# Output projection of a two-layer trunk: seven block products in place of eight, with weight sums made by accumulating transfers

## What is computed

```python
for l in range(DEPTH):                      # DEPTH = 2, S = 512 tokens, D = 1024
    h = rms_norm(x, norm_g[l])
    proj = jnp.einsum('bsd,de->bse', h, w_in[l])
    (a_u, a_v, a_z, b_q, b_k, b_v, b_z, i_q, i_k, i_w, g_a, g_b) = split_columns(proj)
    y_a = spatial_gating_branch(...)        # gated MLP over blocks of 128 positions
    y_b = sparse_attention_branch(...) * jax.nn.silu(b_z)
    o_a = jnp.einsum('bse,ed->bsd', y_a, w_oa[l])
    o_b = jnp.einsum('bse,ed->bsd', y_b, w_ob[l])
    merged = jax.nn.sigmoid(g_a + gate_b[l, 0]) * o_a + jax.nn.sigmoid(g_b + gate_b[l, 1]) * o_b
    x = x + jnp.einsum('bsd,de->bse', merged, w_out[l])     # the output projection: (512 x 1024) by (1024 x 1024)
```

## Time and profile before

| | |
|---|---|
| median of 3 runs | 811.78 us (810.96 to 811.89) |
| the profiled execution, its own time | 811.18 us |
| its span, first to last instruction | 809.4 us |
| TensorE busy | 791.1 us, 98% |
| VectorE busy | 552.2 us, 68% |
| ScalarE busy | 335.9 us, 42% |
| HBM traffic | 104 GB/s over the span |

### The profile page before, as it was taken

How to read it: one execution, slowest core, us unless ns; L and a number is a source line. 1 busy time by engine, 2 the same in 40 slices (tenths; PEclk the granted TensorE clock), 3 DMA queues, 4 the chain that set the end, 5 groups by cost and what they waited for, 6 DMA issues and landing times.

```text
span 809.4 us, 10691 instructions
## 1 busy us (share of the span) xinstructions
PE 791.1 (98%) x3868; PEld 665.5 (82%) x3868; DVE 552.2 (68%) x987; ACT 335.9 (42%) x642; POOL 91.3 (11%) x85
## 2 busy tenths in 40 slices
PE   3999999999999999999999999999999999999998
PEld 2988888888888888888889888888888888888886
DVE  2878999978766753466268799999786567434821
ACT  3656645341444323432254675433324342434400
POOL 1137520000000000000011764000000000000000
PEclk9999999999999999999999999999999999999999
DMA  8535232323233122254062522323322223125211
GB/s 303 183 110 174 82 92 67 103 79 104 78 105 101 47 86 80 95 192 139 32 199 89 183 79 79 104 80 104 102 81 78 82 75 104 53 79 202 84 53 53
DMA packets 38309, 85.26 MB, mean 105 GB/s; under 512 B 2672, under 2 KB 2864, under 8 KB 38256
## 3 DMA queue, kind: packets, MB, share of 16 engines
q1 hardware_dynamic: 34496, 71.31, 27.9%
q0 software_dynamic: 3472, 12.67, 5.0%
q10 hardware_dynamic: 288, 0.59, 0.2%
...
HBM read 78.27 MB, written 6.29 MB: 104 GB/s over the span
## 4 chain that ended last, share of the span: by engine, by line
PE 91%; DVE 6%; DMA 1%; ACT 1%; issue 1%; ACTq 0%; DVEq 0%
PE bank L563 25%; PE bank L561 25%; PE bank L562 25%; PE bank L613 4%; PE bank L535 2%; PE bank L553 2%; PE bank L491 1%; DMA eye<-in_ident 1%; PE bank L544 1%; PE bank L506 1%; PE bank L505 1%; DVE w_lo L920 1%; PE bank L476 1%; DVE index_lo L920 1%; PE bank L647 0%
## 5 line engine op out<-in xcount | busy, mean ns | idle before, releaser
L561 PE MATMUL bank<-h_lo,w_hi 128*128 128x512 f32 x448 | 180.6, 403 | 0.0
L563 PE MATMUL bank<-h_hi,w_hi 128*128 128x512 f32 x448 | 174.7, 390 | 0.0
L562 PE MATMUL bank<-h_hi,w_lo 128*128 128x512 f32 x448 | 174.4, 389 | 0.0
L920 DVE TENSOR_TENSOR w_lo<-w_raw,w_hi 128x1024 fp32r<-128x1024 f32 x120 | 155.4, 1313 | 13.0 <-ACT w_hi L689 8.5
L561 PE MATMUL bank<-w_lo,h_hi 128*128 128x512 f32 x384 | 150.4, 392 | 0.0
L563 PE MATMUL bank<-w_hi,h_hi 128*128 128x512 f32 x384 | 149.8, 390 | 0.0
L562 PE MATMUL bank<-w_hi,h_lo 128*128 128x512 f32 x384 | 149.7, 390 | 0.0
L689 ACT ACTIVATE w_hi<-w_raw 128x1024 fp32r<-128x1024 f32 x120 | 123.2, 1055 | 8.4 <-ACT probs L830 3.7
L562 PEld LDWEIGHTS bank<-h_hi,w_lo 128*128 128x128 f32 x448 | 84.2, 188 | 18.6 <-issue 1.4
L561 PEld LDWEIGHTS bank<-h_lo,w_hi 128*128 128x128 f32 x448 | 84.2, 188 | 18.3 <-issue 1.4
L563 PEld LDWEIGHTS bank<-h_hi,w_hi 128*128 128x128 f32 x448 | 84.1, 188 | 17.9
...
...
## 6 DMA issues: line engine op xcount, KB each, us to landing
w_raw<-in_w_in SPq DMA_DIRECT2D x96, 512.0 KB, 3.7
w_raw<-in_w_out SPq DMA_DIRECT2D x16, 512.0 KB, 3.3
out<-x_sb POOLq DMA_DIRECT2D x4, 1024.0 KB, 5.3
w_raw<-in_w_oa SPq DMA_DIRECT2D x8, 512.0 KB, 3.3
w_raw<-in_w_ob SPq DMA_DIRECT2D x8, 512.0 KB, 3.4
x_sb<-out POOLq DMA_DIRECT2D x2, 2048.0 KB, 8.2
x_sb<-in_x SPq DMA_DIRECT2D x4, 512.0 KB, 9.7
...
```

The source lines that it names most:

```text
L561: nc.tensor.matmul(dst, s_h, m_l, start=(n == 0), stop=False)
L562: nc.tensor.matmul(dst, s_l, m_h, start=False, stop=False)
L563: last = nc.tensor.matmul(dst, s_h, m_h, start=False, stop=(n == len(pairs) - 1))
L920: nc.vector.tensor_tensor(lo, w_raw[:, n % RAW], hi.bitcast(F32), ALU.subtract) \
```

## The change

With the merged matrix A in four blocks (tokens 0 to 255 and 256 to 511, by inner rows 0 to 511 and 512 to 1023) and the weights B in four blocks of 512 x 512, the output is made from seven block products instead of eight, in Winograd's form of Strassen's scheme. In the names of the program: a11 and a12 take blocks of A as they are, s5, s6, s3 and s4 take sums and differences of blocks of A, and a22 again a block. In the order a11, a12, s5, s6, s3, s4, a22 each product is two jobs of 12 matmuls (one for each tile of its 256 tokens), so out has 14 jobs, which I number 0 to 13. Some are added into a bank that an earlier product left there, and so wait until VectorE has read it: s6 on s5, s3 on a11, s4 on s3, a22 on s4.

The sums of weights are made in `w_raw`. A product has two units of 512 KB. The units of a11, a12 and s6 are loaded by SyncE as before; those of s5, s3, s4 and a22 are transfers issued by GpSimd that add the block from HBM to what the slot still holds. Each goes out when the remainder of the unit four before it has been written. Unit numbers below are those of the program: 56 and 57 are a11's, 58 and 59 a12's, 60 and 61 s5's, and so on to 69.

The sums of A are made by VectorE in operations of 256 columns inside `merged_lo`, and split by ScalarE and VectorE (`s5_rounded`, `s5_remainder`, `sum_rounded`, `sum_remainder`). The tile order becomes 1, 0, 3, 2, and the x of two tiles, not one, is transposed for the next layer inside the out group.

```diff
 TILES = SEQ // P
-ORDER = [*range(1, TILES), 0]
+ORDER = [1, 0, 3, 2]
...
+PRODUCTS = ["a11", "a12", "s5", "s6", "s3", "s4", "a22"]
+W_BLOCK = {"a11": (0, 0), "a12": (1, 0), "s5": (0, 1), "s6": (1, 1), "s3": (1, 1), "s4": (0, 1), "a22": (1, 0)}
+W_ADDS = {"s5", "s3", "s4", "a22"}
+W_HOME = {"a11": (0, 0), "a12": (0, 1), "s5": (1, 0), "s6": (1, 1), "s3": (0, 0), "s4": (1, 0), "a22": (1, 1)}
+SUM_BANK = {"a11": (2, 1), "a12": (7, 3), "s5": (5, 6), "s6": (5, 6), "s3": (2, 1), "s4": (2, 1), "a22": (2, 1)}
+OPENS = {"a11", "a12", "s5"}
+GOES_TO = {"a11": (0, 0, 1), "a12": (0, 0, 1), "s5": (1, 1, -1), "s6": (0, 1, -1), "s3": (0, 1, -1), "s4": (1, 1, -1),
+           "a22": (1, 0, 1)}
+HALF_K = KD // 2
+OUT_G = len(GROUPS) - 1
+OUT_U = OUT_G * NQ
+UNITS = OUT_U + 2 * len(PRODUCTS)
...
+def job_of(name, pos):
+    return PLAIN + 2 * PRODUCTS.index(name) + pos
+def tiles_of_job(n):
+    i, pos = divmod(n - PLAIN, 2)
+    name = PRODUCTS[i]
+    low, half, sign = GOES_TO[name]
+    return name, pos, 2 * low + 1 - pos, half, sign
...
+                for u in range(OUT_U, UNITS):
+                    if unit_adds(u):
+                        slot = raw_slot(layer, u)
+                        pool.wait_ge(s_wlo.sem, s_wlo.at(layer, u - RAW + 1))
+                        pool.dma_start(w_raw[:, slot], out_weights(layer, u), accum_op=ALU.add) \
+                            .then_inc(s_wadd[slot], 16)
                 poo.end_layer(pool)
...
+            def out_job(layer, n):
+                name, pos, t, half, _ = tiles_of_job(n)
+                dst = bank[SUM_BANK[name][pos]]
+                tok = slice((1 - pos) * P, (2 - pos) * P)
+                if name == "a11":
+                    b = SUM_BANK[name][pos]
+                    pe.wait_ge(s_free[b].sem, s_free[b].at(layer, BANK_USES[b] - 1))
+                elif name == "a12":
+                    pe.wait_ge(s_yb.sem, s_yb.at(layer, TILES))
+                elif name != "s5":
+                    before = dict(s6="s5", s3="a11", s4="s3", a22="s4")[name]
+                    pe.wait_ge(s_res.sem, s_res.at(layer, job_of(before, pos) - PLAIN + 1))
+                (w_hi, w_lo), w_k = out_home(name)
+                a_hi, a_lo = left_operand(name)
+                for k in range(HALF_K):
+                    if pos == 0 and k % 2 == 0:
+                        pe.wait_ge(s_wlo.sem, s_wlo.at(layer, OUT_U + 2 * PRODUCTS.index(name) + k // 2 + 1))
+                    if name == "a11":
+                        pe.wait_ge(s_mlo.sem, s_mlo.at(layer, k + 1))
+                    elif name == "a12":
+                        pe.wait_ge(s_mlo.sem, s_mlo.at(layer, HALF_K + k + 1))
+                    elif name == "s5":
+                        pe.wait_ge(s_s5lo.sem, s_s5lo.at(layer, k + 1))
+                    elif name in SUMS and k == 0:
+                        pe.wait_ge(s_slo3.sem, s_slo3.at(layer, SUMS.index(name) + 1))
+                    wk, first = w_k.start + k, k == 0 and name in OPENS
+                    nc.tensor.matmul(dst[:], a_hi[:, k, tok], w_lo[:, wk], start=first, stop=False, skip_group_check=True)
+                    nc.tensor.matmul(dst[:], a_lo[:, k, tok], w_hi[:, wk], start=False, stop=False, skip_group_check=True)
+                    last = nc.tensor.matmul(dst[:], a_hi[:, k, tok], w_hi[:, wk], start=False, stop=(k == HALF_K - 1),
+                                            skip_group_check=True)
+                last.then_inc(s_job.sem, 1)
...
@@ -840,14 +1014,23 @@
                     act.wait_ge(s_sum.sem, s_sum.at(layer, d + 1))
                     if d == 0:
                         act.wait_ge(s_job.sem, s_job.at(layer, JOB_GB[-1] + 1))
-                    nc.scalar.activation(h_hi[:, d], g_b[:, d], ACT.Copy, scale=0.5).then_inc(s_mhi.sem, 1)
+                    part = h_hi[:, d], g_b[:, d]
+                    if d < HALF_K:
+                        part = top(h_hi, d), top(g_b, d)
+                    nc.scalar.activation(*part, ACT.Copy, scale=0.5).then_inc(s_mhi.sem, 1)
+                    if d > HALF_K:
+                        s5_rounded(layer, d - HALF_K - 1)
+                if n == JOB_OUT[0]:
+                    s5_rounded(layer, HALF_K - 1)
...
                 dve.wait_ge(s_mhi.sem, s_mhi.at(layer, d + 1))
+                if d < HALF_K:
+                    op = nc.vector.scalar_tensor_tensor(top(h_lo, d), top(g_b, d), 0.5, top(h_hi, d).bitcast(F32),
+                                                        ALU.mult, ALU.subtract)
+                    op.then_inc(s_mlo.sem, 1)
+                    vec.mark(nc.vector.tensor_tensor(s4_raw[:, d], top(g_b, d), bottom(g_b, d), ALU.subtract))
+                    return
+                k = d - HALF_K
                 nc.vector.scalar_tensor_tensor(h_lo[:, d], g_b[:, d], 0.5, h_hi[:, d].bitcast(F32),
                                                ALU.mult, ALU.subtract).then_inc(s_mlo.sem, 1)
+                vec.join(dve)
+                nc.vector.tensor_tensor(bottom(g_b, k), bottom(g_b, d), bottom(g_b, k), ALU.subtract) \
+                    .then_inc(s_s5.sem, 1)
+                dve.wait_ge(s_s5.sem, s_s5.at(layer, k + 1))
+                dve.wait_ge(s_mlo.sem, s_mlo.at(layer, d + 1))
+                vec.link(dve, nc.vector.tensor_tensor(top(g_b, k), bottom(g_b, k), top(g_b, k), ALU.add))
+                op = nc.vector.tensor_tensor(top(g_b, d), top(g_b, k), top(g_b, d), ALU.subtract)
+                if k == HALF_K - 1:
+                    vec.link(dve, op)
+                    dve.sem_inc(s_s6.sem, 1)
+                else:
+                    vec.mark(op)
+            def s5_remainder(layer, k):
+                dve.wait_ge(s_s5hi.sem, s_s5hi.at(layer, k + 1))
+                nc.vector.scalar_tensor_tensor(bottom(h_lo, k), bottom(g_b, k), 0.5, bottom(h_hi, k).bitcast(F32),
+                                               ALU.mult, ALU.subtract).then_inc(s_s5lo.sem, 1)
+            def sum_remainder(layer, name):
+                hi, lo = left_operand(name)
+                dve.wait_ge(s_shi3.sem, s_shi3.at(layer, SUMS.index(name) + 1))
+                nc.vector.scalar_tensor_tensor(lo, raw_sum(name), -0.5 if name == "s3" else 0.5, hi.bitcast(F32),
+                                               ALU.mult, ALU.subtract).then_inc(s_slo3.sem, 1)
             def evacuate(layer, n):
...
@@ -1069,20 +1292,28 @@
                     vec.link(dve, nc.vector.scalar_tensor_tensor(g_b[:, d], g_b[:, d], 1.0, src[:], ALU.add, ALU.mult))
                     dve.sem_inc(free.sem, 1)
                     nc.vector.tensor_tensor(g_b[:, d], g_b[:, d], g_a[:, d], ALU.add).then_inc(s_sum.sem, 1)
+                    if d > HALF_K + 1:
+                        s5_remainder(layer, d - HALF_K - 2)
                     if d:
                         merged_lo(layer, d - 1)
                     if d == KD - 1:
                         merged_lo(layer, d)
+                        s5_remainder(layer, HALF_K - 2)
+                        s5_remainder(layer, HALF_K - 1)
                 elif n in JOB_OUT:
-                    i = n - JOB_OUT[0]
-                    t, half = ORDER[i % TILES], i // TILES
+                    name, pos, t, half, sign = tiles_of_job(n)
                     dve.wait_ge(s_job.sem, s_job.at(layer, n + 1))
-                    if i == 0:
+                    if n == PLAIN:
                         dve.wait_ge(s_xback.sem, s_xback.at(layer, 16))
                     part = x_sb[:, t, half * W512:(half + 1) * W512]
-                    vec.link(dve, nc.vector.tensor_tensor(part, part, src[:], ALU.add))
-                    dve.sem_inc(free.sem, 1)
-                    dve.sem_inc(s_res.sem, 1)
+                    b = SUM_BANK[name][pos]
+                    if n - PLAIN >= 2:
+                        dve.wait_ge(s_res.sem, s_res.at(layer, n - PLAIN - 1))
+                    nc.vector.tensor_tensor(part, part, bank[b][:], ALU.add if sign > 0 else ALU.subtract) \
+                        .then_inc(s_res.sem, 1)
+                    if name == "a22":
+                        dve.wait_ge(s_res.sem, s_res.at(layer, n - PLAIN + 1))
+                        dve.sem_inc(s_free[b].sem, 1)
             def ln_apply(layer, t):
...
@@ -1183,22 +1415,32 @@
                             done[b] += 1
                 for n in range(NJOBS):
-                    if n + 1 < TILES:
+                    if n + 1 < TILES and (n or not layer):
                         h_remainder(layer, n + 1)
                     if n + 2 < TILES:
                         x_normalised(layer, n + 2)
                     if n - 1 in AFTER_QI:
                         index_remainder(layer, AFTER_QI[n - 1])
-                    for g, qt in quarters_in(n, "vector"):
-                        remainder(layer, g, qt)
+                    for u in quarters_in(n, "vector"):
+                        remainder(layer, u)
+                    if n == JOB_OUT[0]:
+                        for name in SUMS:
```

(21 more changed lines are left out.)

226 lines of the change are left out of this document (160 added, 66 removed).

## The result

The changed kernel takes 820.02 us (median of 4 runs, 819.04 to 821.69), the kernel before 811.84 us beside it. The ratio is 1.0101, with a 95% interval of 1.0084 to 1.0117: slower by 8.2 us. The profiled execution took 819.04 us, its span is 817.0 us.

A forecast was written before the change was run, and what follows sets the result against it. TensorE was taken as the bound, with VectorE almost full in ob. −10.9 + 2 × 5.0 + 2.1 + 0.3 + 1.0 = +2.5 us on 811.18 gives 813.7, as a median 814.3 us; eight-in-ten range 808 to 826.

The forecast's parts named there:

- my own case: The main forecast for the whole kernel, 814.3 us, with its own range 811 to 817.5 and a chance of 0.45.
- the rival on transfers: Accumulating transfers in out set the pace: 820 at 8.2 us each, 828 or so if also one by one; chance 0.25.
- What is removed: Out has 168 matmuls for 192 a layer: 5.44 us less a layer, 10.9 us in both.
- VectorE's chain and the first wait: VectorE's added 256-column work from ob into out finishes unit 61 at 384.0, so TensorE waits 3.3 us at s5.
- The second wait: In out, job 6 waits 1.7 us a layer for VectorE's residual of job 4.
- slow return: Rival: TensorE runs slowly after its 3.3 us wait in out, +3.3 us in all, 817.6; chance 0.12.
- The transfers: Accumulating transfers in out land after 6.3 us where 5.7 is free: about 0.5 us a layer, +1.0.
- The seam: Between the layers, VectorE's work makes TensorE wait: 2.0 + 0.5 + 0.8, less 1.2 before, net +2.1 us.
- the wait of job 12: At the seam, job 12 waits 0.5 us for the residual behind the first normalised tile.
- the h_lo of the third tile: At the seam, the new tile order gives less cover, costing 0.8 us for this h_lo.
- The tile order: The new order in layer 0 costs nothing if the first tiles are ready, 1.0 at worst; taken as 0.3 us.

The follow-up runs named there:

- r3_ranked_seam_plain: r2_ranked_seam with plain transfers in place of accumulating ones on GpSimd's queue, so another output: 804.22 us, ratio 0.9911.
- s1_late: Changed kernel with VectorE's three remainders of sums moved behind the weights wanted first, and ScalarE's rounding of unit 61 one job earlier: 815.00 us.
- c1_filler: Changed kernel with thirteen matmuls into an unread bank ahead of TensorE's wait for the second half of s5's weights: 819.68 us.
- b1_gap3: Kernel before the change, with out job 4 of each layer made to wait for three linked VectorE operations on a scratch tile: 821.55 us, ratio 1.0122.
- s2_late_plain: s1_late with plain transfers in place of accumulating ones, so another output: 808.57 us, ratio 0.9957.
- t1_plain: Changed kernel with the eight accumulating transfers a layer made plain on the same GpSimd queue, so another output: 812.76 us, ratio 1.0009.
- r2_ranked_seam: Changed kernel with VectorE's steps in out ordered by TensorE's need and the small index weights handled earlier at the layer seam, accumulating transfers kept: 811.55 us.

## Why the prediction was right in sign and small in size

I forecast 814.3 us and slower; it is 820.0 and slower. That is inside my eight-in-ten range of 808 to 826 and outside the 811 to 817.5 of my own case. It is the time that I had worked out for the rival on transfers, and that is luck: the rival had it from a landing of 8.2 us for each transfer, and the median measured is 6.5.

- **What is removed** stands: 336 matmuls in out, 0.2267 us apart where the clock is full. With every known hindrance taken off but one wait of 2.5 us and the seam, the time is 7.9 us under the kernel before beside 10.9 (r3_ranked_seam_plain).
- **VectorE's chain and the first wait** stand: the prediction had ob job 5 over at 367.6, job 7 at 377.6, unit 61 done at 384.0 and a wait of 3.3 us; the rows are 367.70, 377.71, 384.07 and 3.08 us (3.10 in layer 1). Its cause, the three remainders of sums ahead of unit 61, is shown by VectorE's rows above and by s1_late.
- **The second wait** of 1.7 us does not show, although residual 4 came when predicted (389.87 for 389.8). TensorE was still in job 5, because it ran at half speed. Where its clock was kept up, 1.41 us of wait appeared (c1_filler). I had priced slow return as a rival of 1.6 us a layer that adds to both waits; it is 2.9 us, and takes the second wait's place, so it costs 1.2 us net up to job 6. That idling brings it on is shown by c1_filler in both layers, and by b1_gap3 in one layer of two; the same wait in its other layer cost nothing, so idling is not the whole of it.
- **The transfers** are the step that failed: the term of 1.0 us, "about 0.5 us a layer". The landing time that I took, 6.3 us, was near the median of 6.5. But I asked only how late one transfer may be and not how many can pass: out wants one unit per job of 2.72 us, and an accumulating transfer fills all 16 engines for 3.0 us, so a series of five falls behind by itself, to 10.3 us. The rival had this thought (one by one at 4 us) and I gave it 828 and too little weight. (The 828 does not come out of its terms either: 6.4 us a layer more is 826 on my sum without the 1.0, and 833 on the 820.) In place of 1.0 us the runs show 6.4 us at equal clock (s1_late against s2_late_plain), and 7.3 us twice with a shorter slow stretch in it (t1_plain; r2_ranked_seam against r3_ranked_seam_plain). The prediction's sum without this term is +1.5 us; t1_plain has +0.8.
- The estimate of 3.2 us from the Trainium skill, "DMA: Bandwidth & Descriptors", section "Anatomy of one DMA", is refuted for this form: 6.5 us in the median. For a plain load of the same queue the median in t1_plain was 4.5 us, and the shortest 3.7.
- **The seam** was priced at 2.1 us. Its wait of 1.97 us shows, and half of it went with plain transfers (1.03 in t1_plain); the wait of job 12 was 1.17 us for 0.5. The 0.8 us for the h_lo of the third tile does not show: the whole index stage is only 0.4 us longer.
- **The tile order** in layer 0: 45.57 for 45.84 at the first matmul of the next stage. Nothing; I had 0.3.

With 5.4 us of matmuls taken off and a second transpose added in layer 0, out is 9.2 us longer than it should be there and 7.8 in layer 1; the rows of the waits and the 2.9 us give 8.0 and 7.3. Most of the rest is in how the rows count. A wait counts from the end of the matmul before it, 0.39 us after that one's start, where the next would have started after 0.23; and at full clock the matmul behind a wait is followed after 0.34 us (405.94, 406.28 in the timeline). Over the three waits and the two these make 0.7 and 0.4 us.

What stays open: why one wait lowers the clock and another of the same length does not, and why the slow matmuls behind waits of 3.1 to 3.3 us last 3.4 us in one place and 6.1 in another.
